# Layer 1 latent keys on token rows: squares, roots and scaling by token, then transposes, with both key slots ahead of the query pairs

## The chip, the cores and the metric

One core of a Trainium2 chip runs the program. The metric is the device time of one execution in microseconds, lower is better. The median of three runs of the kernel before is 1565.3 us (1560.97 to 1568.23).

## What is computed

Two layers of a hybrid backbone over 256 latent and 256 context tokens of 2048 channels. Layer 0 joins windowed attention and a long convolution, layer 1 joins dense grouped attention with multi-head latent attention (MLA). The change is in the keys of MLA, which for latent tokens and context tokens are

```
kv  = (rmsnorm(mkv, ckv_g) @ wukv).reshape(B, L, 8, 128 + 128)   # per head: key part, value part
k_n = rmsnorm(kv[..., :128], mk_g[:128])                          # over the 128 channels of one head, per token
k   = concat([k_n, broadcast(k_r)])                               # k_r: 64 rotated channels, shared by the heads
s   = (q . k) * 192 ** -0.5 ;  o = softmax(s) @ kv[..., 128:]
```

The queries come in the same way from a 512-channel latent, in four pairs of heads, each with a normalised part (qn) and a rotated part (qr). All results are multiplied with a SiLU gate and go through an output projection.

## The kernel before

All tensors are f32. Each product of weights and activations is made of three fp32r products of high and low halves: `split_high` (ScalarE, L979) copies a loaded weight tile `raw` to `wh`, `split_low` (VectorE, L989) makes `wl` as the difference. `raw`, `wh` and `wl` have two buffers each, so tile t+1 is split while tile t is multiplied, and a load (SP queue) starts when the tile two before it is split.

Layer 1 is a hand-written order of `L1_TILES` = 41 slots, one weight tile each. The function `l1_slot(i)` names the fills of a slot; a fill is one accumulation in bank 0 or 1 (`ps[m % 2]`). Every engine walks the slots and does its own part: TensorE the fills, the sums of squares (`sums`), the attention pieces; ScalarE the split of the next tile, the drains of the banks, the roots, exponentials and copies; VectorE the low split, reciprocals, scalings and the softmax. A fill into a bank waits for the drain of the fill two before it (`odd_drained`).

Slots 0 to 18 are the latents, the grouped keys, values and queries and the query latent (cq). From `MLA0` = 19 to slot 30 odd slots hold MLA fills and even slots one gate tile each: slot 19 is kn 0 to 3 and vm 0 to 3 (keys and values of four heads), slots 21 and 23 query pairs 0 and 1, slot 25 the other four heads' keys and values, slots 27 and 29 query pairs 2 and 3. Slots 31 to 40 are gates. `MLA_SLOTS` gives the slot in which each MLA head's attention (units 8 to 15) has its scores; its transposes follow one slot later, its outputs two.

A key fill before (kind kn) has a head's 128 channels on the partitions and 512 tokens on the free axis. So the sum over channels is a product with ones on TensorE. Four heads share one norm: `sums` (L2040) puts the sums of head n on 16 rows of bank 7, one root (L2184) and one reciprocal (L2275, 128x512) serve the four, and `pick` (L2051) is a product that spreads one head's row over all partitions of bank 7, from which `scale_kn` (L2290) scales the key. `PICK_LAG` = 6 sets how many fills later. Bank 7 is shared by the sums, the picks and the swaps of the rotations (`swap`, L2060), so these wait for each other's readers. The latent cq's norm closes at the first fill of slot 19, so its root, its four scalings (L2283) and its splits `cqh` and `cql` (L2243, L2355) fall into that slot.

## Time and profile before

| | |
|---|---|
| median of three runs | 1565.3 us (1560.97 to 1568.23) |
| profiled execution | 1564.63 us, span 1562.8 us |
| TensorE busy | 1482.5 us, 95% |
| VectorE busy | 1025.4 us, 66% |
| ScalarE busy | 575.9 us, 37% |
| mean granted TensorE clock | 0.984 of 2.4 GHz |
| layer 1's slots 19 to 40 | 1235.69 to 1461.35 us of the span |
| output projection of layer 1 | from there to the end |

Times inside the span are counted from its start. TensorE's busy time is modelled at its ends: a matmul's record is longer than the spacing of two, so prices are read from start to start. A whole f32 matmul appears as two records, an fp32r one as one.

### The profile page before, as it was taken

How to read it: one execution, taken by the hardware profiler on the slowest of the kernel's cores; microseconds unless marked ns; L12 is line 12 of the kernel's file. 1: busy time of each engine (PE TensorE's matmuls, PEld its weight loads, DVE VectorE, ACT ScalarE, POOL GpSimd, SP SyncE). 2: the span in 40 equal slices, each digit the busy share in tenths (PEclk: the TensorE clock that was granted, in tenths of full speed). 3: DMA queues.
4: the chain of work that ended last, by engine and by line, in shares of the span. 5: the costliest groups of instructions: out<-in, count | busy, mean ns of one | idle time of the engine just before them, and what ended most of it. 6: DMA issues, size and time to landing. Idle time of an engine off the chain costs nothing.

```text
span 1562.8 us, 19306 instructions
## 1 busy us (share of the span) xinstructions
PE 1482.5 (95%) x7755; PEld 1181.3 (76%) x7755; DVE 1025.4 (66%) x1199; ACT 575.9 (37%) x806; POOL 214.7 (14%) x242
## 2 busy tenths in 40 slices
PE   5978999999999999999998999989999988999998
PEld 1325888888888787788776888877788775788998
DVE  3373898889897876876666545464577465565543
ACT  2543222222222334433234211253367545555332
POOL 1000333322231100000000334430000000000000
PEclk9998999999999999999999999989999999999999
DMA  9996554554654544452548666522232322233563
GB/s 356 380 363 239 205 180 167 166 192 148 216 175 153 200 150 154 135 196 93 193 160 307 211 226 207 190 95 89 101 126 91 101 75 75 74 109 121 193 220 141
DMA packets 72904, 272.29 MB, mean 174 GB/s; under 512 B 11056, under 2 KB 25584, under 8 KB 53104
## 3 DMA queue, kind: packets, MB, share of 16 engines
q1 hardware_dynamic: 52640, 193.45, 35.2%
q0 software_dynamic: 20176, 77.61, 14.3%
q8 instruction: 62, 1.02, 0.3%
q14 instruction: 26, 0.21, 0.0%
HBM read 256.36 MB, written 14.68 MB: 173 GB/s over the span
## 4 chain that ended last, share of the span: by engine, by line
PE 82%; DMA 6%; DVE 4%; ACT 4%; issue 3%; SPq 0%; ACTq 0%; DVEq 0%; POOL 0%
PE banks L1027 20%; PE banks L1028 20%; PE banks L1031 20%; DMA raw<-in_ev_tiles 2%; PE banks L1198 2%; PE banks L1185 2%; PE banks L2110 2%; DMA ada_ring<-in_ada_first 2%; ACT wh L979 1%; DMA spectra<-kstage 1%; PE banks L2040 1%; PE banks L1001 1%; PE banks L538 1%; PE banks L1004 1%; PE banks L1002 1%
## 5 line engine op out<-in xcount | busy, mean ns | idle before, releaser
L1027 PE MATMUL banks<-xh,wh 128*128 128x512 f32 (+1 forms) x1808 | 619.3, 358 | 7.2 <-ACT wh L979 7.2
L1028 PE MATMUL banks<-xl,wh 128*128 128x512 f32 (+1 forms) x1808 | 604.4, 350 | 0.0
L1027 PEld LDWEIGHTS banks<-xh,wh 128*128 128x128 f32 x1808 | 342.8, 190 | 60.7 <-issue 15.9
L1028 PEld LDWEIGHTS banks<-xl,wh 128*128 128x128 f32 x1808 | 343.0, 190 | 46.2 <-issue 3.1
L1031 PE MATMUL banks<-xh,wl 128*128 128x512 f32 (+1 forms) x1808 | 354.9, 349 | 0.0
L989 DVE TENSOR_TENSOR wl<-raw,wh 128x2048 fp32r<-128x2048 f32 (+1 forms) x124 | 281.3, 2269 | 88.1 <-ACT wh L979 88.1
L1031 PEld LDWEIGHTS banks<-xh,wl 128*128 128x128 f32 x1808 | 295.9, 189 | 43.6
L979 ACT ACTIVATE wh<-raw 128x2048 fp32r<-128x2048 f32 (+1 forms) x124 | 235.5, 1900 | 239.5 <-PE banks L1031 169.2
L373 DVE SCALAR_TENSOR_TENSOR ada_acc<-ada_w,cond,ada_acc 128x1024 f32<-128x1024 f32 x120 | 159.3, 1328 | 6.0 <-DMA ada_w<-in_ada_rest 3.9
L396 POOL DMA_DIRECT2D ada_w<-in_ada_rest x128 | 69.0, 539 | 586.8 <-DVE ada_acc L385 390.0
L385 DVE SCALAR_TENSOR_TENSOR ada_acc<-ada_w,cond,ada_acc 128x1024 f32<-128x1024 f32 x90 | 125.3, 1392 | 0.0
L2275 DVE RECIPROCAL rs<-rs 128x256 f32<-128x256 f32 (+1 forms) x27 | 56.9, 2107 | 56.9 <-ACT rs L2184 56.7
L1818 DVE SCALAR_TENSOR_TENSOR hT<-banks,ada,hres 128x256 f32<-128x256 f32 x48 | 21.7, 480 | 103.0 <-PE banks L1031 102.4
L1342 ACT ACTIVATE cx<-banks,cols 128x512 f32<-128x512 f32 x16 | 12.5, 778 | 147.4 <-PE banks L1031 147.4
L1160 POOL TENSOR_TENSOR spec<-spec,prod 128x512 f32<-128x512 f32 x32 | 47.5, 1510 | 55.4 <-DVE prod L1500 55.4
L538 PE MATMUL banks<-ada_ring,condw 128*32 128x512 f32 x256 | 36.0, 645 | 14.0 <-DMA ada_ring<-in_ada_first 9.2
L2309 DVE TENSOR_REDUCE mx<-banks 128x2 f32<-128x1024 f32 x16 | 19.6, 1223 | 32.1 <-PE banks L2090 24.3
L2040 PE MATMUL banks<-sq,core 128*128 128x256 f32 (+1 forms) x74 | 29.3, 478 | 11.7 <-ACT sq L2176 4.7
L1001 PE MATMUL banks<-xh,wh 128*128 128x512 f32 x64 | 27.1, 423 | 14.0 <-DVE wl L989 11.3
L1402 ACT ACTIVATE prob<-banks,nb,qscale 128x512 f32<-128x512 f32 (+1 forms) x32 | 21.2, 667 | 44.4 <-DVE nb L1581 44.4
L2193 ACT ACTIVATE prob<-banks,nb 128x512 f32<-128x512 f32 x32 | 21.7, 684 | 37.1 <-DVE nb L2311 37.1
L1375 ACT ACTIVATE th<-banks 128x512 f32<-128x512 f32 x16 | 9.5, 591 | 66.0 <-PE banks L1031 66.0
(293 smaller groups left out, 1621.9 us busy)
## 6 DMA issues: line engine op xcount, KB each, us to landing
ada_w<-in_ada_rest POOLq DMA_DIRECT2D x128, 512.0 KB, 3.8
raw<-in_ev_tiles SPq DMA_DIRECT2D x52, 1024.0 KB, 6.4
raw<-in_od_tiles SPq DMA_DIRECT2D x34, 1024.0 KB, 4.8
ada_ring<-in_ada_first SPq DMA_DIRECT2D x32, 1024.0 KB, 11.0
raw<-in_out_tiles SPq DMA_DIRECT2D x32, 1024.0 KB, 5.2
hT<-in_hT POOLq DMA_DIRECT2D x4, 1024.0 KB, 11.0
spectra<-kstage POOLq DMA_DIRECT2D x4, 1024.0 KB, 10.5
kf<-spectra SPq DMA_DIRECT2D x8, 512.0 KB, 5.6
```

The lines of the kernel that those rows point to most:

```text
L373: ins = nc.vector.scalar_tensor_tensor(out=acc[:, 0, :], in0=w, scalar=b.cond[:, k, 0:1], in1=acc[:, 0, :], op0=ALU.mult, op1=ALU.add)
L385: ins = nc.vector.scalar_tensor_tensor(out=acc[:, 1, :], in0=w, scalar=b.cond[:, k, 1:2], in1=acc[:, 1, :], op0=ALU.mult, op1=ALU.add)
L396: pool.dma_start(b.ada_w[:, p % 2, :], ada_rest[p // KT, p % KT]).then_inc(s.ada_landed[p % 2], 16)
L538: last = nc.tensor.matmul(ps[7][32 * q:32 * q + 32, :], b.condw[:, 4 * r + q, :], b.ada_ring[p % ADA_RING][:, q // 2, q % 2, :], start=(r ...
L979: nc.scalar.activation(b.wh[:, t % 2, 0:width], b.raw[:, t % 2, 0:width], ACT.Copy).then_inc(s.hi_done, 1)
L989: nc.vector.tensor_tensor(b.wl[:, t % 2, 0:width], b.raw[:, t % 2, 0:width], b.wh[:, t % 2, 0:width].bitcast(F32), ALU.subtract).then_inc( ...
L1027: nc.tensor.matmul(out, wh[:, k, :], b.xh[:, seg, k, :], start=(k == 0), stop=False)
L1028: nc.tensor.matmul(out, wh[:, k, :], b.xl[:, seg, k, :], start=False, stop=False)
L1031: last = nc.tensor.matmul(out, wl[:, k, :], b.xh[:, seg, k, :], start=False, stop=(k == KT - 1))
L1160: nc.gpsimd.tensor_tensor(b.spec[:, j], b.spec[:, j], b.prod[:, j % 2, :].rearrange("p (v c) -> p v c", v=2), ALU.subtract if j % 2 == 0 e ...
L2040: nc.tensor.matmul(ps[7][:, 0:width], lhs.get(kind, b.ones), b.sq1[:, (count_fills(m, NORMED) - 1) % 2, 0:width], start=first, stop=closes ...
L2275: v.reciprocal(b.rs1[:, 0:width], b.rs1[:, 0:width]).then_inc(s.odd_rstd, 1)
```

## The change

- `l1_slot` gives key fills the kind kt: fill kt 4*half + t has the 128 tokens of tile t on the partitions and the channels of four heads side by side on the free axis (tokens as the stationary side, as the value fills have it). The sums (L2040) and picks (L2051) of the keys are gone, and GROUPED has no kn.
- ScalarE copies the bank to `ktok[t]` (which lies in the place of `kn` for heads 4 to 7) and squares it to `sqk`, one buffer. VectorE reduces the squares of each head to one column (`key_squares`, into `kss`). After four tiles ScalarE takes the root of 16 columns (`key_roots`), VectorE the reciprocal, and scales the four tiles by a broadcast of the columns (`scale_keys`).
- TensorE turns the 16 blocks of 128x128 into banks 4 to 7 (`turn_keys`) and ScalarE copies them to `kn` with the gain as scale (`keep_keys`), in the slot after.
- `MLA_AT` sets the order: keys in slots 19 and 21, query pairs in 24, 26, 28 and 30; gates in 20, 22, 23, 25, 27, 29 and from 31. The turns stand at the end of slots 20 and 22. `MLA_SLOTS` goes from (24, 25, 26, 28, 30, 32, 34, 36) to (27, 28, 29, 30, 31, 33, 35, 36).

```diff
     b.cq = put("cq", "U", 20 * K, [P, 4, 256])
+    b.ktok = [b.kn[:, 4 + t, :] for t in range(4)]
+    b.sqk = put("sqk", "U", 62 * K, [P, 512])
+    b.kss = put("kss", "V", 2432, [P, 16])
+    b.krk = put("krk", "V", 2496, [P, 16])
     b.cqh = put("cqh", "U", 24 * K, [P, 4, 256], F32R)
...
 T1 = OUT0 + OUT_TILES
-MLA0 = 19
-NORMED = ("ckv", "kr", "k", "q", "cq", "kn", "qn", "qr")
-PICK_LAG = 6
+MLA_AT = {19: ("k", 0), 21: ("k", 1), 24: ("q", 0), 26: ("q", 1), 28: ("q", 2), 30: ("q", 3)}
+KEY_TURN = {20: 0, 22: 1}
+NORMED = ("ckv", "kr", "k", "q", "cq", "qn", "qr")
 ROTATED = ("kr", "k", "q", "qr")
-GROUPED = {"ckv": 2, "cq": 4, "kn": 4}
+GROUPED = {"ckv": 2, "cq": 4}
 MEAN = {"ckv": 256, "cq": 512, "kr": 64, "qr": 64}
...
         return [("cq", i - 15, 256)]
-    if i < MLA0 + 12 and (i - MLA0) % 2 == 0:
-        half, r = divmod((i - MLA0) // 2, 3)
-        if r == 0:
-            return [("kn", 4 * half + n, T) for n in range(4)] + [("vm", 4 * half + n, T) for n in range(4)]
-        pair = 2 * half + r - 1
-        return [("qn", 2 * pair, 256), ("qn", 2 * pair + 1, 256), ("qr", pair, 256)]
+    if i in MLA_AT:
+        side, n = MLA_AT[i]
+        if side == "k":
+            return [("kt", 4 * n + t, T) for t in range(4)] + [("vm", 4 * n + t, T) for t in range(4)]
+        return [("qn", 2 * n, 256), ("qn", 2 * n + 1, 256), ("qr", n, 256)]
     return [("gate", l1_gate(i), 256)]
...
-    if i >= MLA0 + 12:
-        return i - MLA0 - 6 if i < L1_TILES else None
-    return (i - MLA0) // 2 if i > MLA0 and (i - MLA0) % 2 else None
+    if i < min(MLA_AT) or i in MLA_AT or i >= L1_TILES:
+        return None
+    return i - min(MLA_AT) - sum(at < i for at in MLA_AT)
...
-def group_end(m):
-    return fill_is(m, ("kn",)) and FILLS[m][1] % 4 == 3
 def hurried(m):
...
-MLA_SLOTS = (24, 25, 26, 28, 30, 32, 34, 36)
+MLA_SLOTS = (27, 28, 29, 30, 31, 33, 35, 36)
...
     kind, n, _ = l1_slot(i)[0]
-    if kind == "kn":
+    if kind == "kt":
         return g.od_wukv[0, :, 256 * n:256 * n + 1024].rearrange("(k p) n -> p k n", p=P), (2, 1024)
...
         return b.qo[:, 8 + n, :]
-    return {"ckv": b.ckv, "k": b.kgqa, "v": b.vpre1, "q": b.qo, "cq": b.cq, "kn": b.kn, "qr": b.qr}[kind][:, n, :]
+    return {"ckv": b.ckv, "k": b.kgqa, "v": b.vpre1, "q": b.qo, "cq": b.cq, "qr": b.qr}[kind][:, n, :]
...
                 pe.wait_ge(s.odd_drained, m - 1)
-            if kind in ("kn", "vm", "qn", "qr"):
+            if kind in ("kt", "vm", "qn", "qr"):
                 pe.wait_ge(s.hi_done, t + 1)
                 pe.wait_ge(s.lo_done, t + 1)
-            if kind in ("kn", "vm"):
+            if kind in ("kt", "vm"):
                 pe.wait_ge(s.ckv_high, 2)
...
                     for k in range(2):
-                        if kind == "kn":
-                            lhs, rhs, out = w[wp][:, k, 256 * (n % 4):256 * (n % 4) + P], xp[:, k, :], bank
-                        else:
-                            lhs = xp[:, k, P * (n % 4):P * (n % 4) + P]
-                            rhs = w[wp][:, k, :].rearrange("p (h c) -> p h c", h=4)[:, :, P:2 * P]
-                            out = bank.rearrange("p (h c) -> p h c", h=4)
+                        lhs = xp[:, k, P * (n % 4):P * (n % 4) + P]
+                        side = slice(0, P) if kind == "kt" else slice(P, 2 * P)
+                        rhs = w[wp][:, k, :].rearrange("p (h c) -> p h c", h=4)[:, :, side]
+                        out = bank.rearrange("p (h c) -> p h c", h=4)
                         ins = nc.tensor.matmul(out, lhs, rhs, start=(c == 0 and k == 0), stop=(c == 2 and k == 1))
...
                     pe.wait_ge(s.odd_swap_used, swaps_before(m + 1))
-                if count_fills(m - 1, ("kn",)):
-                    last = max(j for j in range(m) if fill_is(j, ("kn",)))
-                    pe.wait_ge(s.odd_normed, count_fills(last, NORMED))
-            lhs = {"kr": b.blocks64, "qr": b.blocks64, "kn": b.batch[:, 112 - 16 * (n % 4):240 - 16 * (n % 4)]}
+                if kind == "qn":
+                    pe.wait_ge(s.odd_kread, 10)
+            lhs = {"kr": b.blocks64, "qr": b.blocks64}
             nc.tensor.matmul(ps[7][:, 0:width], lhs.get(kind, b.ones),
...
-        def pick(m):
-            n = FILLS[m][1]
-            last = m + 3 - n % 4
-            pe.wait_ge(s.odd_rstd, count_norms(last))
-            if n % 4:
-                pe.wait_ge(s.odd_normed, count_fills(m - 1, NORMED))
-            nc.tensor.matmul(ps[7], b.pick[:, n % 4, :], b.rs1[:], start=True, stop=True).then_inc(s.odd_pick, 1)
+        def turn_keys(half):
+            if half == 0:
+                pe.wait_ge(s.odd_out, 8)
+                pe.wait_ge(s.odd_probT, 8)
+                pe.wait_ge(s.odd_root, count_norms(FIRST_FILL[min(MLA_AT)] - 1))
+                pe.wait_ge(s.odd_swap_used, swaps_before(FIRST_FILL[min(MLA_AT)]))
+            else:
+                pe.wait_ge(s.odd_kread, 6)
+            for t in range(4):
+                pe.wait_ge(s.odd_kmade, 9 * half + 6 + t)
+                for h in range(4):
+                    last = nc.tensor.transpose(ps[4 + t][:, P * h:P * h + P], b.ktok[t][:, P * h:P * h + P], b.ident)
+                last.then_inc(s.odd_kturned, 1)
...
                 pe.wait_ge(s.odd_kr, 1)
+                pe.wait_ge(s.odd_kread, 10)
             if u > 0:
...
                     fill(i, m)
-                if fill_is(m - PICK_LAG, ("kn",)) and not group_end(m - PICK_LAG):
-                    pick(m - PICK_LAG)
                 for r in rotated_at(m):
...
                 scores(l1_unit(i))
-            if group_end(FIRST_FILL[i + 1] - PICK_LAG):
-                pick(FIRST_FILL[i + 1] - PICK_LAG)
+            if i in KEY_TURN:
+                turn_keys(KEY_TURN[i])
             for m in rotated_at(FIRST_FILL[i]):
...
                 return
-            if (kind, n) == ("kn", 0):
+            if (kind, n) == ("kt", 0):
...
                 act.wait_ge(s.odd_scored, 8)
+            if kind == "kt":
+                half, t = divmod(n, 4)
+                if half:
+                    act.wait_ge(s.odd_kturned, t + 1)
+                a.activation(b.ktok[t], bank, ACT.Copy).then_inc(s.odd_kcopied, 1)
+                if n:
+                    act.wait_ge(s.odd_kmade, 9 * half + t if t else 4)
+                a.activation(b.sqk[:], bank, ACT.Square).then_inc(s.odd_drained, 1)
+                return
             if kind not in NORMED:
...
             a.activation(b.sq1[:, q % 2, 0:width], bank, ACT.Square).then_inc(s.odd_drained, 1)
+        def key_roots(half):
+            act.wait_ge(s.odd_kmade, 9 * half + 4)
+            a.activation(b.krk[:], b.kss[:], ACT.Sqrt, scale=1.0 / 128, bias=b.small[:, 0:1]).then_inc(s.odd_kread, 1)
+        def keep_keys(half):
+            for t in range(4):
+                act.wait_ge(s.odd_kturned, 4 * half + (4 if half else t + 1))
+                a.activation(b.kn[:, 4 * half:4 * half + 4, P * t:P * t + P],
+                             ps[4 + t].rearrange("p (h t) -> p h t", h=4), ACT.Copy,
+                             scale=b.cols[:, COL["mk_n"]:COL["mk_n"] + 1]).then_inc(s.odd_kread, 1)
...
                     root(m - 1)
+                if fill_is(m - 2, ("kt",)) and FILLS[m - 2][1] % 4 == 3:
+                    key_roots(FILLS[m - 2][1] // 4)
                 if fill_is(m - 2, ("ckv", "cq")) and closes_norm(m - 2):
...
                 gated_high(l1_gate(i - 1))
+            if i - 1 in KEY_TURN:
+                keep_keys(KEY_TURN[i - 1])
             for m in rotated_at(FIRST_FILL[i - 1]) if i else ():
...
             v.reciprocal(b.rs1[:, 0:width], b.rs1[:, 0:width]).then_inc(s.odd_rstd, 1)
-            if kind == "kn":
-                return
             dve.wait_ge(s.odd_rstd, count_norms(m))
...
-        def scale_kn(m):
-            n = FILLS[m][1]
-            dve.wait_ge(s.odd_pick, n + 1)
-            dve.wait_ge(s.odd_kept, count_fills(m, NORMED))
-            v.scalar_tensor_tensor(out=b.kn[:, n, :], in0=b.kn[:, n, :], scalar=b.cols[:, COL["mk_n"]:COL["mk_n"] + 1],
-                                   in1=ps[7], op0=ALU.mult, op1=ALU.mult).then_inc(s.odd_normed, 1)
+        def key_squares(m):
+            half, t = divmod(FILLS[m][1], 4)
+            dve.wait_ge(s.odd_drained, m + 1)
+            if half and t == 0:
+                dve.wait_ge(s.odd_kread, 1)
+            v.tensor_reduce(b.kss[:, 4 * t:4 * t + 4], b.sqk[:].rearrange("p (h c) -> p h c", h=4), AX.X,
+                            ALU.add).then_inc(s.odd_kmade, 1)
+        def scale_keys(half):
+            dve.wait_ge(s.odd_kread, (1, 2)[half])
+            v.reciprocal(b.krk[:], b.krk[:]).then_inc(s.odd_kmade, 1)
+            dve.wait_ge(s.odd_kmade, 9 * half + 5)
+            dve.wait_ge(s.odd_kcopied, 4 * half + 4)
+            for t in range(4):
+                x = b.ktok[t].rearrange("p (h c) -> p h c", h=4)
+                v.tensor_tensor(x, x, b.krk[:, 4 * t:4 * t + 4].unsqueeze(2).to_broadcast([P, 4, P]),
+                                ALU.mult).then_inc(s.odd_kmade, 1)
...
             for m in range(FIRST_FILL[i], FIRST_FILL[i + 1]):
-                if fill_is(m - PICK_LAG, ("kn",)) and not group_end(m - PICK_LAG):
-                    scale_kn(m - PICK_LAG)
+                if fill_is(m - 1, ("kt",)):
+                    key_squares(m - 1)
+                if fill_is(m - 3, ("kt",)) and FILLS[m - 3][1] % 4 == 3:
+                    scale_keys(FILLS[m - 3][1] // 4)
                 for r in rotated_at(m):
...
                 gated_low(l1_gate(i - 1))
-            if group_end(FIRST_FILL[i + 1] - PICK_LAG):
-                scale_kn(FIRST_FILL[i + 1] - PICK_LAG)
             for m in rotated_at(FIRST_FILL[i]):
```

Three places show how instructions stand. TensorE, the start of slot 19, before (`wh`, `wl`: weight halves, `ckvh`, `ckvl`: latent halves, `sq` with `core`: a sum of squares):

```order
L2007 MATMUL banks<-ckvl,wh 128x512 x2
L2007 MATMUL banks<-ckvh,wl 128x512 x2
L2040 MATMUL banks<-sq_158,core 128x256
L2007 MATMUL banks<-ckvh,wh 128x512 x2
L2007 MATMUL banks<-ckvl,wh 128x512 x2
L2007 MATMUL banks<-ckvh,wl 128x512 x2
L2040 MATMUL banks<-sq_158,core 128x512
L2007 MATMUL banks<-ckvh,wh 128x512 x2
L2007 MATMUL banks<-ckvl,wh 128x512 x2
```


and with the change:

```order
L2003 MATMUL banks<-wh,ckvl 128x512 x2
L2003 MATMUL banks<-wl,ckvh 128x512 x2
L2035 MATMUL banks<-sq_158,core 128x256
L2003 MATMUL banks<-wh,ckvh 128x512 x2
L2003 MATMUL banks<-wh,ckvl 128x512 x2
L2003 MATMUL banks<-wl,ckvh 128x512 x2
L2003 MATMUL banks<-wh,ckvh 128x512 x2
L2003 MATMUL banks<-wh,ckvl 128x512 x2
L2003 MATMUL banks<-wl,ckvh 128x512 x2
```


The sum of cq's squares stays behind the first fill; the sums of 512 columns between the key fills are gone, and fill follows fill.

ScalarE, slot 19, before (`kn`: the copy of a key fill, `sq`: its square, `rs`: the root of cq's norm, `cqh`: high halves of cq):

```order
L2172 ACTIVATE kn<-banks 128x512
L2176 ACTIVATE sq_158<-banks 128x512
L2184 ACT_TABLE_LOAD
L2184 ACTIVATE rs_151<-banks,small 128x256
L2172 ACTIVATE kn<-banks 128x512
L2176 ACTIVATE sq_158<-banks 128x512
L2243 ACTIVATE cqh<-cq 128x256 x4
L2172 ACTIVATE kn<-banks 128x512
L2176 ACTIVATE sq_158<-banks 128x512
L2172 ACTIVATE kn<-banks 128x512
L2176 ACTIVATE sq_158<-banks 128x512
```


and with the change, where each square but the first waits for `key_squares` on VectorE:

```order
L2173 ACTIVATE kn<-banks 128x512
L2176 ACTIVATE sqk<-banks 128x512
L2204 ACT_TABLE_LOAD
L2204 ACTIVATE rs_151<-banks,small 128x256
L2173 ACTIVATE kn<-banks 128x512
L2176 ACTIVATE sqk<-banks 128x512
L2265 ACTIVATE cqh<-cq 128x256 x4
L2173 ACTIVATE kn<-banks 128x512
L2176 ACTIVATE sqk<-banks 128x512
L2173 ACTIVATE kn<-banks 128x512
L2176 ACTIVATE sqk<-banks 128x512
```


The order is the same, the square's buffer is now `sqk`, and the waits differ.

ScalarE, from the gate of slot 20 to the first query pair in slot 21, before:

```order
L2160 ACT_TABLE_LOAD
L2160 ACTIVATE silu_153<-banks 128x256
L2161 ACTIVATE silu_153<-banks 128x256
L979 ACTIVATE wh<-raw 128x2048
L2172 ACTIVATE qo<-banks 128x256
L2176 ACTIVATE sq_158<-banks 128x256
L2172 ACTIVATE qo<-banks 128x256
```


and with the change from the gate of slot 23 to the first query pair in slot 24:

```order
L983 ACTIVATE wh<-raw 128x1536
L2160 ACTIVATE silu_153<-banks 128x256
L2161 ACTIVATE silu_153<-banks 128x256
L2238 ACTIVATE xh<-qo 128x256
L2194 ACTIVATE kn<-banks,cols 128x4x128 x4
L983 ACTIVATE wh<-raw 128x2048
L2181 ACTIVATE qo<-banks 128x256
L2185 ACTIVATE sq_158<-banks 128x256
L2181 ACTIVATE qo<-banks 128x256
L2185 ACTIVATE sq_158<-banks 128x256
```


The copies of the second half's keys (L2194) stand between the gate's drain and the split of the next tile (L983), behind which the first query fill is drained.

## Rows read from the trace of the kernel before

**Rows 1.** The page, part 1: busy time, share of the span, instructions of each engine.

```profile
PE 1482.5 (95%) x7755; PEld 1181.3 (76%) x7755; DVE 1025.4 (66%) x1199; ACT 575.9 (37%) x806; POOL 214.7 (14%) x242
```

**Rows 2.** Windows: length, PE, PEld, DVE, ACT, POOL busy (instructions), PEclk, DMA, GB/s.

```profile
1235.69:1260.02 24.33, 20.39 (x73) 13.98 (x71) 11.99 (x13) 13.00 (x21) 0.00 (x0) 0.93 0.24 74
...
1303.55:1328.84 25.29, 20.66 (x78) 13.00 (x77) 10.85 (x14) 13.93 (x21) 0.00 (x0) 1.00 0.18 62
1328.84:1384.17 55.33, 51.62 (x318) 42.67 (x317) 35.95 (x45) 32.52 (x59) 0.00 (x0) 0.97 0.27 91
1384.17:1461.35 77.18, 77.18 (x570) 70.12 (x568) 44.34 (x62) 38.87 (x63) 0.00 (x0) 1.00 0.36 125
```

**Rows 3.** Timeline of TensorE, slot 19: start, us, operation, count, [idle before <-releaser].

```profile
1234.89 1.04 PE L2100 MATMUL banks<-core,prob 128*128 128x128 f32 x8
1235.69 0.71 PE L2007 MATMUL banks<-ckvh,wh 128*128 128x512 f32 x2
...
1250.08 1.02 PE L2040 MATMUL banks<-sq,core 128*128 128x512 f32 x2
...
1251.41 0.62 PE L2007 MATMUL banks<-wh,ckvl 128*128 128x512 f32 x2
1251.87 0.62 PE L2007 MATMUL banks<-wl,ckvh 128*128 128x512 f32 x2
```

**Rows 4.** Timeline of TensorE, slots 19 to 27: the waits, and two pairs in between.

```profile
1241.65 1.45 PE L2040 MATMUL banks<-sq,core 128*128 128x512 f32 x2 [2.51 <-issue]
...
1243.75 1.06 PE L2007 MATMUL banks<-ckvl,wh 128*128 128x512 f32 x2
1244.60 1.06 PE L2007 MATMUL banks<-ckvh,wl 128*128 128x512 f32 x2
...
1255.27 1.13 PE L2051 MATMUL banks<-rs,core 128*128 128x512 f32 x2 [1.43 <-DVE rs L2275]
...
1267.91 1.10 PE L2051 MATMUL banks<-rs,core 128*128 128x512 f32 x2 [0.93 <-DVE kn L2290]
...
1308.79 1.12 PE L2040 MATMUL banks<-sq,core 128*128 128x512 f32 x2 [2.15 <-ACT sq L2176]
...
1321.88 1.12 PE L2051 MATMUL banks<-rs,core 128*128 128x512 f32 x2 [2.48 <-DVE rs L2275]
...
1346.76 0.67 PE L2040 MATMUL banks<-sq,core 128*128 128x256 f32 x2 [1.75 <-DVE kn L2290]
```

**Rows 5.** Timeline of VectorE, slot 19: the scaling of cq.

```profile
1243.38 1.67 DVE L2283 SCALAR_TENSOR_TENSOR cq<-cq,cols,rs 128x256 f32<-128x256 f32 x4
```

**Rows 6.** Groups by line and shape, VectorE and ScalarE, whole span: busy, mean ns, idle before.

```profile
L1573 DVE TENSOR_REDUCE mx<-banks 128x2 f32<-128x512 f32 x8 | 5.5, 684 | 1.9 <-PE banks L1254 1.9
...
L821 DVE TENSOR_TENSOR xl<-nu,xh 128x512 fp32r<-128x512 f32 x16 | 11.1, 692 | 0.5
...
L979 ACT ACTIVATE wh<-raw 128x2048 fp32r<-128x2048 f32 x120 | 229.6, 1913 | 239.5 <-PE banks L1031 169.2 <-DMA raw<-in_ev_tiles 50.4 <-DMA spectra<-kstage 12.2
```

**Rows 7.** Timeline of ScalarE, slot 19.

```profile
1239.79 1.28 ACT L2184 ACT_TABLE_LOAD   x1
...
1241.45 0.59 ACT L2172 ACTIVATE kn<-banks 128x512 f32<-128x512 f32 x1
...
1245.08 1.33 ACT L2243 ACTIVATE cqh<-cq 128x256 fp32r<-128x256 f32 x4 [2.55 <-DVE cq L2283]
```

**Rows 8.** Timeline of TensorE: the swap behind slot 22, and slot 29's first sum to last.

```profile
1284.17 1.22 PE L2060 MATMUL banks<-qr,core 128*128 128x256 f32 x2 [2.87 <-DVE qr L2283]
...
1368.25 0.89 PE L2040 MATMUL banks<-sq,core 128*128 128x256 f32 x2 [1.96 <-ACT sq L2176]
...
1371.51 0.83 PE L2040 MATMUL banks<-sq,core 128*128 128x256 f32 x2
```

**Rows 9.** Timeline of VectorE, unit 10 in slot 28: the maximum and the scaled probabilities.

```profile
1362.84 1.22 DVE L2309 TENSOR_REDUCE mx<-banks 128x2 f32<-128x1024 f32 x1 [1.73 <-PE banks L2090]
...
1365.99 0.88 DVE L2316 TENSOR_SCALAR prob<-prob,rden 128x512 f32<-128x512 f32 x2
```

More of the change, by code:

```diff
@@ L2452, in semaphores @@
     s.odd_out = sem("odd_out")
-    s.odd_pick = sem("odd_pick")
+    s.odd_kcopied = sem("odd_kcopied")
+    s.odd_kmade = sem("odd_kmade")
+    s.odd_kread = sem("odd_kread")
+    s.odd_kturned = sem("odd_kturned")
     s.odd_prob = sem("odd_prob")
```

## The prediction

> **What bounds the kernel now.** I read the page first: TensorE is busy for 1482.5 us, 95% of the span, VectorE for 66% and ScalarE for 37% [rows 1]. So only work taken off TensorE, or TensorE's own waits, can move the time. Next the windows, cut at the edges of layer 1's slots: idle is length less PE busy [rows 2]. Slot 19 (keys and values of heads 0 to 3) takes 24.33 us with 3.9 idle, slot 25 with slot 26's attention pieces (heads 4 to 7) 25.29 with 4.6 idle, slots 27 to 30 lose 3.7 of 55.33. From slot 31 on nothing is idle in 77.18 us. The change touches the two latent key slots and the order of the slots up to 30; behind them TensorE is the bound and passes on whatever was won.
>
> **What goes from TensorE.** The eight L2040 sums of 512 columns and the eight L2051 picks. At full clock L2040 starts at 1250.08 and the pair behind the next one at 1251.41: 1.33 us for it and one L2007 pair, and a pair alone takes 0.46 (1251.41 to 1251.87). So an f32 matmul of 512 columns costs 0.87 us [rows 3]; the picks have the same shape. 16 x 0.87 = 13.9 us.
>
> **What comes to TensorE.** 32 transposes of 128x128. Eight of the kernel's L2100 transposes take 0.80 us from start to the next operation's start (1234.89 to 1235.69) [rows 3], 0.10 each: 3.2 us. Net work: 13.9 - 3.2 = **-10.7 us**. The kt fills are the same six matmuls of 512 columns as the kn fills, with the operands' sides exchanged as the vm fills have them; L2007 has the same spacing in both forms, so they cost nothing.
> The Trainium skill (TensorE: Matmul & The Clock Gate, "Part 4: PE-mode transpose") gives about 275 ns for one transpose in a kernel. By that the 32 would cost 8.8 us and the net would be -5.1; the row's 0.10 us decides, and the rule is rival 3.
>
> **Waits that go.** (a) Slot 19: the sum of kn 0 stood behind the root of the last cq on bank 7 (2.51 us idle before 1241.65), and the clock was then at 1.2 GHz: a pair took 0.85 (1243.75 to 1244.60) instead of 0.46, some 1.5 us over the three fills' pairs that ran slow [rows 4, 3]. The first pick waited 1.43 for the reciprocal. (b) Slot 20: 0.93 before the fourth pick. (c) Slot 25: 2.15 before a sum and 2.48 before a pick. (d) Slot 27: 1.75 before qn's sum, which waited for the last key scaling [rows 4]. Together **-12.8 us**.
>
> **Waits that come.** (e) *Slot 19.* sqk is one buffer, so ScalarE's square of kt 1 waits until VectorE has reduced the square of kt 0, and that reduce is queued behind the cq normalise, whose four scalings end at 1243.38 + 1.67 = 1245.05 [rows 5]. A reduce of 128x512 to four columns: the nearest row is 0.68 [rows 6]. ScalarE copies the second key tile at 1241.45 as before, stands to about 1245.75 for the square, is done at 1246.3, and makes the four cqh (1.33 us) [rows 7]. TensorE meanwhile: kt 2 needs kt 0's drain, whose square is over when the table load behind it starts at 1239.79 [rows 7], and ends at 1241.2 (three pairs of 0.46); kt 3 needs kt 1's drain. So TensorE idles about 0.8 and then **5.1 us**, and restarts at 1246.4 at the slow clock (the 2.51 us gap here was enough for that). kt 3 slow takes 2.7, to 1249.1; kt 2's square, behind the cqh and a reduce, lets vm 0 go at 1249.5 and costs 0.5, and vm 0 half slow 0.6. Then vm 1, 2, 3 at 1.4 each and the outputs of unit 7 with 1.7 (four f32 matmuls of 256 columns, half of 0.87 each) put gate 0 at 1257.5, where it stood at 1260.02 [rows 2]. Stalls here: 7.0 us.
> (f) *Slot 21.* ScalarE and VectorE alternate: square 0.5, reduce 0.65, two handovers of 0.1, against 1.37 of TensorE a fill. About 0.4 at kt 7's bank, another 0.4 behind: 0.8 us. The DVE reciprocal of 16 columns replaces one of 512 (3.35) and the scalings of four tiles (nearest row 0.69 each [rows 6]) end before turn_keys: slot 20's and slot 22's gates (48 matmuls of 256 columns at 0.12, half of 0.23, 5.8 us each) cover root, reciprocal and scalings, about 3.5 us. turn_keys(1) also needs keep_keys(0), 4 x 0.5 on ScalarE at the head of slot 22: ready some 2.5 us early. If that cover went, it would cost 1 to 3.
> (g) *Slot 24*, the first query pair. ScalarE leaves gate 2 at 1290.6 by my walk and then makes xh (0.3, a quarter of the four cqh), the four keep_keys (2.0, near four of the 0.59 copies of rows 7, which overlap a little as the cqh do) and the split of the next tile (1.9 [rows 6]) before it drains qn 0 with 0.55, at 1295.4. TensorE, with gate 2 ended at 1290.0, has filled qn 0 and qn 1 (24 matmuls at 0.12) by 1292.9: 2.5 us idle, then slow. The price of a slow stretch after such a gap is in slot 29: 1368.25 to 1371.51 at the slow clock, 3.26 us, of which I count 1.3 as lost [rows 8]. 2.5 + 1.3 = 3.8.
> (h) *Slot 28*, the third pair, now follows a slot with exponentials (unit 8), as slot 29 did before (1.96 idle, then slow [rows 8]): 3.2 us. Slot 30 does the same as slot 29 before: no change. The swap behind the first pair, with no attention to cover it, still waits 2.87 [rows 8]: moved to slot 25, no change.
> Together e to h: 7.0 + 0.8 + 3.8 + 3.2 = **+14.8 us**.
>
> **The other moves.** Units 8 to 15 go to slots 27 to 36, later and denser. No SP transfer is added; tiles load in the new order, each when the split two tiles earlier is done, and slots 22 and 23 as gates give them time. POOL has no part in it. ScalarE gains four table loads net (1.28 us each [rows 7], 5.1 in all); they lie in slots 26 to 31. There ScalarE has, by my count, about 18 us of work in each 22 us of TensorE: I cost them at nothing, unless that cover is gone (rival 2).
>
> **Sum.** -10.7 - 12.8 + 14.8 = **-8.7 us**; the small waits inside the first pair that (g) swallows make it **-9**. The profiled execution took 1564.6 (span 1562.8 and 1.8 around it), 0.7 under the median of 1565.3. 1564.6 - 9 = 1555.6; against the median 1556.3. I say **1556**. About 0.5% (7.8 us) is what a measurement of this kernel can tell from no change; the bound for faster is 1557.5.
> Bounds. Low: if (e) idles only the 2.5 us it had before and (h) does not come, -15. High: if (e), (g) and (h) each last 2 us more, -3.
>
> **The rivals.**
> *1. The stalls take the gain back.* The wait (e) grows since the clock stays low over the value fills too, and (g) and (h) are each a full slow stretch as behind the swap at 1284.17. For it: three new waits, each on ScalarE. Against: TensorE loses 13.9 us of work for certain. -3, so 1562.
> *2. Slower: dense units.* Slots 27 to 31 carry a unit each. If the chain from the maximum to the scaled probabilities (1362.84 to 1365.99 + 0.88, 4.0 us [rows 9]), now with table loads between, is not covered, TensorE waits for it at the transposes: five slots x 4.0 = 20, so -9 + 20 = +11, 1576. It decides when less than 4.0 us of TensorE work, plus 1.3 for a load, stands between scores and transposes. Against: a gate gives 5.8, a pair 5.2 (36 matmuls at 0.12 and two sums at 0.43), and three units in a row in slots 24 to 26 had no such wait.
> *3. Dear transposes.* If a key transpose takes 0.28 us and not 0.10, 32 of them give back 5.6: 1561. The transposed operand is the moving one in both, so I hold it unlikely.
> *4. Cheap waits.* The clock does not fall and (e) is short: 1550.
> That the change would not do what it says is no case: the order shows the sums and picks gone.
>
> **Chances.** Forecast (1553 to 1560) 0.60, rival 1 0.22, rival 2 0.06, rival 3 0.05, rival 4 0.07. Faster by over 0.5%: three quarters of the forecast's case and rival 4, 0.52. Slower: rival 2 and a little, 0.07. Same: 0.41. The range 1550 to 1563 leaves out rival 2 and some of the ends.
>
> **What would show it.** In the new profile: no f32 matmul of 512 columns in the key slots beside the fills; two groups of 16 transposes of 0.1 us; gate 0's product at about 1257.5; a gap near 5 us in slot 19 before the fourth key fill, released by the square; a gap near 2.5 us in slot 24; slot 21 at about 11.5 us where slot 25 had some 21.6 without attention. I am wrong if slot 19 ends later than 1260, if slot 21 has gaps over 2 us, or if the slots from 32 on show idle.

## The result and the profile after

The changed kernel takes **1552.77 us** (median of six runs, 1550.41 to 1556.17), the kernel before, run beside it, 1564.97: a ratio of 0.9926 with a 95% interval of 0.9906 to 0.9945. The forecast was 1556 (1550 to 1563). The profiled executions took 1564.63 and 1556.17.

The page's first line, which answers to [rows 1]:

```profile
PE 1473.7 (95%) x7755; PEld 1177.9 (76%) x7755; DVE 1024.1 (66%) x1207; ACT 585.2 (38%) x818; POOL 217.0 (14%) x242
```

TensorE has 8.8 us less of busy time and the same share. The two profiled executions differ by less than the medians, since the profiled execution of the change came 2.9 us later to slot 19 (1238.63, before 1235.69), before any changed instruction; in the profiles below this point lies between 1233.95 and 1238.17. So I compare the stretch from the first key fill of slot 19 to the first matmul of the output projection. Windows of that stretch, before and after (columns as in [rows 2]):

```profile
1235.69:1462.10 226.41, 207.51 (x1277) 172.83 (x1275) 131.86 (x161) 123.87 (x206) 0.00 (x0) 0.97 0.30 99
```

```profile
1238.63:1453.53 214.90, 197.65 (x1277) 169.85 (x1274) 130.43 (x169) 132.93 (x218) 0.00 (x0) 0.97 0.31 104
1238.63:1260.84 22.21, 16.60 (x62) 12.44 (x59) 12.46 (x19) 12.73 (x21) 0.00 (x0) 0.85 0.25 93
1268.45:1280.32 11.87, 11.65 (x52) 8.64 (x50) 5.59 (x8) 8.82 (x15) 0.00 (x0) 1.00 0.37 115
```

It went from 226.41 to **214.90 us, 11.5 less**, which is nearly the difference of the medians (12.2). Slot 19 took 22.21 where it took 24.33 [rows 2], the second key slot 11.87 alone where it took 25.29 with 3.7 us of attention in it. TensorE waits in slot 19 in fewer places, but longer. Its timeline there:

```profile
1242.76 0.73 PE L2003 MATMUL banks<-wh,ckvh 128*128 128x512 f32 x2 [0.68 <-ACT sqk L2176]
...
1243.79 0.62 PE L2003 MATMUL banks<-wl,ckvh 128*128 128x512 f32 x2
1249.27 1.22 PE L2003 MATMUL banks<-wh,ckvh 128*128 128x512 f32 x2 [4.86 <-ACT sqk L2176]
1250.28 1.06 PE L2003 MATMUL banks<-wh,ckvl 128*128 128x512 f32 x2
1251.14 1.06 PE L2003 MATMUL banks<-wl,ckvh 128*128 128x512 f32 x2
...
1266.78 1.91 PE L2051 MATMUL banks<-core,kn 128*128 128x128 f32 x16
1268.45 0.70 PE L2003 MATMUL banks<-wh,ckvh 128*128 128x512 f32 x2
```

The wait of 4.86 us stands before the fourth key fill, and the clock is at its lower level behind it: a pair takes 0.86 us (1250.28 to 1251.14), where it took 0.46 at 2.4 GHz [rows 3], and the mean granted clock of the slot is 0.85, where it was 0.93 [rows 2]. The 16 turns take 1.67 us, 0.104 each. The waits of the query pairs in slots 24, 28 and 30, and of the swap in slot 25:

```profile
1299.53 1.01 PE L2035 MATMUL banks<-sq,core 128*128 128x256 f32 x2 [2.84 <-ACT sq L2185]
...
1312.70 0.70 PE L2061 MATMUL banks<-qr,core 128*128 128x256 f32 x2 [2.87 <-DVE qr L2305]
...
1335.45 0.67 PE L2035 MATMUL banks<-sq,core 128*128 128x256 f32 x2 [1.84 <-ACT sq L2185]
...
1359.25 0.67 PE L2035 MATMUL banks<-sq,core 128*128 128x256 f32 x2 [1.97 <-ACT sq L2185]
```

And what ScalarE and VectorE do during the long wait:

```profile
1244.39 0.59 ACT L2173 ACTIVATE kn<-banks 128x512 f32<-128x512 f32 x1
1248.62 0.60 ACT L2176 ACTIVATE sqk<-banks 128x512 f32<-128x512 f32 x1 [3.64 <-DVE kss L2313]
1249.11 1.32 ACT L2265 ACTIVATE cqh<-cq 128x256 fp32r<-128x256 f32 x4
```

```profile
1244.53 1.75 DVE L2299 RECIPROCAL rs<-rs 128x256 f32<-128x256 f32 x1 [0.47 <-ACT rs L2204]
1246.31 1.67 DVE L2305 SCALAR_TENSOR_TENSOR cq<-cq,cols,rs 128x256 f32<-128x256 f32 x4
1247.90 0.68 DVE L2313 TENSOR_REDUCE kss<-sqk 128x4 f32<-128x512 f32 x1
```

ScalarE has copied the second token tile at 1244.39 and stands until 1248.62, since the reduce of the first square (`kss`, at 1247.90, 0.68 us) is behind the reciprocal and the scalings of cq in VectorE's queue.

### The profile page after: what moved, and what is told of

The parts are those of the page before. It is cut to its first block, busy times and chain, and to the rows that moved or that the text cites. A ratio compares the mean times of both kernels' runs of the same rounds, so it can differ in the third digit from the quotient of the medians.

```text
span 1554.3 us, 19313 instructions
## 1 busy us (share of the span) xinstructions
PE 1473.7 (95%) x7755; PEld 1177.9 (76%) x7755; DVE 1024.1 (66%) x1207; ACT 585.2 (38%) x818; POOL 217.0 (14%) x242
## 4 chain that ended last, share of the span: by engine, by line
PE 82%; DMA 6%; ACT 4%; DVE 4%; issue 3%; SPq 1%; DVEq 0%; ACTq 0%; POOL 0%
PE banks L1031 20%; PE banks L1032 20%; PE banks L1035 20%; DMA raw<-in_ev_tiles 2%; PE banks L1202 2%; PE banks L1189 2%; DMA ada_ring<-in_ada_first 2%; PE banks L2112 2%; ACT wh L983 1%; DMA spectra<-kstage 1%; PE banks L1005 1%; PE banks L2035 1%; PE banks L542 1%; PE banks L1008 1%; PE banks L1006 1%
## 5 line engine op out<-in xcount | busy, mean ns | idle before, releaser
L993 DVE TENSOR_TENSOR wl<-raw,wh 128x2048 fp32r<-128x2048 f32 x124 | 281.3, 2269 | 92.0 <-ACT wh L983 92.0
L983 ACT ACTIVATE wh<-raw 128x2048 fp32r<-128x2048 f32 x124 | 235.7, 1901 | 237.1 <-PE banks L1035 170.4
L1822 DVE SCALAR_TENSOR_TENSOR hT<-banks,ada,hres 128x256 f32<-128x256 f32 x48 | 21.8, 481 | 104.0 <-PE banks L1035 103.5
L2299 DVE RECIPROCAL rs<-rs 128x256 f32<-128x256 f32 (+1 forms) x25 | 50.2, 2008 | 41.5 <-ACT rs L2204 41.3
L1005 PE MATMUL banks<-xh,wh 128*128 128x512 f32 x64 | 27.1, 424 | 13.9 <-DVE wl L993 11.2
L1157 POOL TENSOR_TENSOR fold<-cz 128x512 f32<-128x512 f32 x16 | 28.4, 1794 | 34.8 <-DVE cz L1529 25.9
```

The costliest lines, as they stand in the source:

```text
L983: nc.scalar.activation(b.wh[:, t % 2, 0:width], b.raw[:, t % 2, 0:width], ACT.Copy).then_inc(s.hi_done, 1)
L993: nc.vector.tensor_tensor(b.wl[:, t % 2, 0:width], b.raw[:, t % 2, 0:width], b.wh[:, t % 2, 0:width].bitcast(F32), ALU.subtract).then_inc( ...
L1005: nc.tensor.matmul(out, wh[:, k, :], b.xh[:, :, k, :], start=(k == 0), stop=False)
L2299: v.reciprocal(b.rs1[:, 0:width], b.rs1[:, 0:width]).then_inc(s.odd_rstd, 1)
```

## The experiments

Medians of four to ten runs (the change: six); the stretch is that from slot 19's first key fill to the output projection's first matmul, in one profile of each kernel. Two kernels whose intervals overlap are not told apart by their medians. The kernel before, in the runs beside them, had 1564.64 us (the first four), 1565.18 (the next three) and 1566.38 (the last four).

| kernel | us | ratio to before, 95% | stretch us |
|---|---|---|---|
| before | 1564.97 | | 226.41 |
| the change | 1552.77 | 0.9926 (0.9906 to 0.9945) | 214.90 |
| order alone | 1562.38 | 0.9986 (0.9975 to 0.9998) | 224.24 |
| four buffers of squares | 1552.69 | 0.9919 (0.9896 to 0.9942) | 212.76 |
| cq's norm later | 1546.20 | 0.9876 (0.9854 to 0.9899) | 208.64 |
| no norm of the keys | 1544.74 | 0.9877 (0.9854 to 0.9901) | 207.46 |
| key copies earlier | 1549.50 | 0.9903 (0.989 to 0.9917) | 208.61 |
| splits later | 1552.42 | 0.992 (0.9907 to 0.9934) | 214.19 |
| these four together | 1546.23 | 0.9888 (0.987 to 0.9906) | 207.57 |
| rotation earlier | 1554.35 | 0.9931 (0.9916 to 0.9947) | 215.04 |
| rotation earlier, two splits later | 1546.58 | 0.9877 (0.9857 to 0.9897) | 210.86 |
| all mended | 1541.24 | 0.9847 (0.983 to 0.9865) | 202.09 |
| the removed work put back | 1566.99 | 1.0005 (0.9991 to 1.002) | 228.46 |

**The order alone.** The kernel before, keys as they were, with the change's tables:

```diff
-MLA0 = 19
+MLA_AT = {19: ("k", 0), 21: ("k", 1), 24: ("q", 0), 26: ("q", 1), 28: ("q", 2), 30: ("q", 3)}
...
-MLA_SLOTS = (24, 25, 26, 28, 30, 32, 34, 36)
+MLA_SLOTS = (27, 28, 29, 30, 31, 33, 35, 36)
```

> The kernel before with the new order of slots and attention units alone; keys as before (sums, picks, one root of four heads). Theory (the gain is the 10.7 us of TensorE work that went, and the waits only changed places): the key slots keep their waits on bank 7, so about the time before, 1562 to 1568. Rival (the order makes the gain, since both key slots come before the query pairs): 1556 or less.

It took 1562.38. Its stretch:

```profile
1235.13:1459.37 224.24, 206.83 (x1277) 171.48 (x1275) 132.08 (x161) 128.78 (x210) 0.00 (x0) 0.98 0.30 100
```

224.24 us: by the stretch the order gives 2.2 of the 11.5 us, the token keys 9.3. The order's part was not in the sum; it is small, and 1.1 of the 2.2 is a slow stretch of the clock behind the first swap that was shorter in this profile (see "The key copies earlier").

**No norm of the keys.** The same kernel with the order, and the latent keys' norm left out altogether:

```diff
-NORMED = ("ckv", "kr", "k", "q", "cq", "kn", "qn", "qr")
+NORMED = ("ckv", "kr", "k", "q", "cq", "qn", "qr")
-PICK_LAG = 6
+PICK_LAG = 6000
```

> Leaves the norm of the latent keys out in the kernel with the new order: no squares, sums, roots, picks, scalings or transposes of keys. What it is faster than e1 is the price of the old norm, what it is faster than the change is the price of the new one. Theory: old norm 13.9 us of TensorE work and some 5 of waits, 18 to 20 us over e4; new norm 3.3 us of transposes, 2.4 of key copies before the query pair and 2 of waits, 7 to 8 us over e4, so e4 at 1545. Rival (the token norm is nearly free and the order pays): e4 within 4 us of the change.

1544.74 us, and the stretch is 207.46:

```profile
1233.95:1441.41 207.46, 193.76 (x1246) 166.63 (x1244) 119.82 (x151) 120.55 (x198) 0.00 (x0) 0.97 0.32 108
```

The old norm costs 224.24 - 207.46 = 16.8 us, the new one 214.90 - 207.46 = 7.4. By the medians they are 17.6 and 8.0. The new one is as expected (7 to 8), the old one a little under 18 to 20. In this profile the stretch behind the first swap was 1.2 us longer than in the two it is compared with, so both prices are rather too small than too large. Even here slot 19 keeps a wait of 3.20 us before the first value fill: the drain of the third key fill is behind the four `cqh`, and these are behind cq's scalings. That part of slot 19's wait belongs to cq, not to the keys:

```profile
1244.73 1.22 PE L2006 MATMUL banks<-wh,ckvh 128*128 128x512 f32 x2 [3.20 <-ACT kn L2169]
```

**The removed work, put back.** 16 f32 matmuls of 512 columns in front of the turns:

```diff
                 pe.wait_ge(s.odd_kmade, 9 * half + 6 + t)
+                for _ in range(2):
+                    nc.tensor.matmul(ps[4 + t], b.ones, b.ktok[t], start=True, stop=True)
```

> The changed kernel with 16 more f32 matmuls of 512 columns, two ahead of each token tile's turn in slots 20 and 22 (their results are overwritten by the turns). It is the work of the eight sums and eight picks that the change took away, at a place without waits. Theory: 16 x 0.87 us, 13.9 us slower than the change, 1566 to 1567. Rival (such work hides behind other engines there): under 7 us.

1566.99 us. That is 14.2 over the change, and the stretch grows by 13.6. Read in place, slot 20's eight and its turns take 8.54 us (1262.16 to 1270.70) where the turns alone took 1.67, so 0.86 for each. The stretch:

```profile
1234.92:1463.38 228.46, 211.55 (x1309) 175.94 (x1307) 130.50 (x169) 132.94 (x218) 0.00 (x0) 0.96 0.30 98
```

So the work of the sums and picks, 0.85 us a matmul here, is on the path in full, and with it the change gains nothing.

**Four buffers for the squares.** `sqk` becomes a list of four, and the square's wait for the reduce falls away in slot 19 (the cut shows the buffers alone).

```diff
-    b.sqk = put("sqk", "U", 62 * K, [P, 512])
+    b.sqk = [put(f"sqk{j}", "U", k * K, [P, 512]) for j, k in enumerate((62, 58, 56, 54))]
```

> The changed kernel with four buffers for the squares, so that ScalarE's square no longer waits for VectorE's reduce. Theory (the 4.86 us wait before the fourth key fill is the queue on VectorE and ScalarE behind the norm of cq): the wait before the fourth fill goes, but the next fill waits for the drain of the third, which is behind the four cqh; 1 to 2 us faster than the change, 1551. Rival (the single buffer is the cause of the wait): 5 us or more, 1548.

1552.69 us, the change's time; the expected gain of 1 to 2 us is not shown. Its stretch is 2.1 us shorter, but only 0.55 of that are waits of slot 19, and slot 19 as a whole differs by up to 1.5 us between profiles of kernels with the same code there (see below). The timeline of TensorE shows the wait cut in two, not gone:

```profile
1245.06 0.73 PE L2003 MATMUL banks<-wh,ckvh 128*128 128x512 f32 x2 [1.11 <-ACT sqk L2176]
...
1249.92 1.22 PE L2003 MATMUL banks<-wh,ckvh 128*128 128x512 f32 x2 [3.20 <-ACT sqk L2176]
```

1.11 before the fourth key fill and 3.20 before the first value fill, the same 3.20 as without any norm. Together they are 4.31 against 4.86: the single buffer held the fourth fill longer, but most of what it held back would have waited here.

**The norm of cq later.** The steps of cq's root, scalings and splits become functions of the fill:

```diff
+def root_step(m):
+    return m + (7 if FILLS[m][0] == "cq" else 1)
+def norm_step(m):
+    return FIRST_FILL[22] if FILLS[m][0] == "cq" else m + 1
```

> The changed kernel with the root of cq's norm put behind the key roots in slot 19, its reciprocal and scalings in slot 22 and its two splits in slot 23; one buffer of squares as in the change. Theory: slot 19 shrinks from 22.2 us to about 16, the 4.86 us wait and the slow clock behind it go; 5 to 7 us faster than the change, 1546. Rival (ScalarE's split and drains bound the slot, and the time comes back later): within 2 us of the change, with the waits in slots 20 to 24.

1546.20 us, 6.6 faster than the change. What is left in slot 19 and what came in slot 24:

```profile
1242.29 0.73 PE L2018 MATMUL banks<-wh,ckvh 128*128 128x512 f32 x2 [0.93 <-ACT sqk L2191]
...
1286.49 0.71 PE L2029 MATMUL banks<-cqh,wh 128*128 128x256 f32 x4 [2.61 <-DVE cql L2407]
```

The 4.86 us are 0.93. cq's low half now lands late for the first query pair and holds it for 2.61, since in slot 23 I had put its splits behind gate 2's drain. That costs almost nothing new: it stands in the place of the change's 2.84 us before the same pair's sum, where no wait is left. TensorE waits a little earlier, and ScalarE works off its key copies and its split meanwhile.

**The key copies earlier.** `keep_keys(1)` goes from the end of slot 23 to behind that slot's split, where ScalarE was idle:

```diff
+            if KEY_TURN.get(i - 1) == 1:
+                keep_keys(1)
...
-            if i - 1 in KEY_TURN:
-                keep_keys(KEY_TURN[i - 1])
+            if KEY_TURN.get(i - 1) == 0:
+                keep_keys(0)
```

> The changed kernel with the second half's four key copies (keep_keys) moved from behind gate 2's drain in slot 23 to ahead of it, where ScalarE stood idle for 5.2 us. Theory: the 2.84 us wait in slot 24 falls to about 0.5, and the slow clock behind it may go: 2.3 to 3.6 us faster than the change, 1549 to 1550.5. Rival (the split of the next tile alone holds the drain): the wait stays over 2 us, no difference.

1549.50 us; the stretch is 6.3 less than the change's, the median 3.3, as expected (2.3 to 3.6), though the two intervals of the table overlap a little. The wait fell as expected, by 2.32:

```profile
1294.79 0.70 PE L2035 MATMUL banks<-sq,core 128*128 128x256 f32 x2 [0.52 <-ACT sq L2185]
...
1306.89 0.70 PE L2061 MATMUL banks<-qr,core 128*128 128x256 f32 x2 [2.87 <-DVE qr L2307]
...
1313.05 0.67 PE L2035 MATMUL banks<-sq,core 128*128 128x256 f32 x2 [0.73 <-issue]
```

The rest is clock. The pair behind the shorter wait runs 1.1 us faster (first sum to swap, 12.10 against 13.17). That belongs to the wait: the three kernels with 0.52 or 0.53 us of it have 12.1 there, the five with 2.83 or 2.84 have 12.9 to 14.4. From the swap to the sum at 1313.05 are 6.16 us; in the change, from the swap at 1312.70 to the sum at 1320.34, 7.64. The wait of 2.87 before the swap is the same in both, and only in the change is there a stretch at 1.2 GHz behind it. The windows, the change's first:

```profile
1312.70:1320.34 7.64, 6.92 (x41) 6.64 (x41) 4.15 (x7) 4.58 (x8) 0.00 (x0) 0.78 0.45 140
```

```profile
1306.89:1313.05 6.16, 5.43 (x41) 5.15 (x41) 4.16 (x7) 4.59 (x8) 0.00 (x0) 1.00 0.47 117
```

These 1.5 us can't be put down to the edit. The order alone and the kernel without a key norm have the short wait in slot 24 too, and take 7.67 and 8.88 us behind the swap. And the kernel with the early rotation (below) keeps the wait of 2.83 and takes 6.16:

```profile
1311.96 0.70 PE L2061 MATMUL banks<-qr,core 128*128 128x256 f32 x2 [2.87 <-DVE qr L2305]
...
1318.12 0.67 PE L2035 MATMUL banks<-sq,core 128*128 128x256 f32 x2 [0.73 <-issue]
```

All thirteen profiles have this swap with its 2.87 us of waiting and the same TensorE work behind it, and from it to the next pair's second sum are 6.16 us in four of them, 7.64 to 7.68 in six and 8.78 to 8.88 in three. The last 1.4 us lie in slot 19, ahead of the edit: with the same code and the same waits it took 22.21 in the change and 20.76 here (20.8 to 22.2 in the six profiles that have this code). So about 3.4 of the 6.3 us are the edit's, which is what the medians show.

**The splits later.** In the pair slots, the split of the next tile goes behind the first two drains and the first root:

```diff
+            pair_slot = FILLS[FIRST_FILL[i]][0] == "qn"
-            if i > 1:
+            if i > 1 and not pair_slot:
                 split_high(nc, act, b, s, t0 + i + 1, width(i + 1))
...
+                if pair_slot and m == FIRST_FILL[i] + 1:
+                    split_high(nc, act, b, s, t0 + i + 1, width(i + 1))
```

> The changed kernel where, in the four query pair slots, the split of the next weight tile stands behind the drains of the first two fills and the first root (ScalarE) or its reciprocal (VectorE). Theory: the waits of 1.84 and 1.97 us in slots 28 and 30 go, and the one in slot 24 falls from 2.84 to about 1: 4 to 7 us faster than the change, 1547. Rival (the split is then late for the next gate, or the roots wait instead): under 2 us, with a new wait at the gate's first product.

1552.42 us, no gain: this expectation was wrong in slots 28 and 30. Slot 24's wait did fall, from 2.84 to 1.03. TensorE's timeline:

```profile
1297.00 0.36 PE L1031 MATMUL banks<-xh,wh 128*128 128x256 f32 x1 [1.17 <-ACT wh L983]
...
1315.82 0.36 PE L1031 MATMUL banks<-xh,wh 128*128 128x256 f32 x1 [1.17 <-ACT wh L983]
...
1332.01 0.67 PE L2035 MATMUL banks<-sq,core 128*128 128x256 f32 x2 [1.82 <-DVE rope L2337]
...
1355.40 0.67 PE L2035 MATMUL banks<-sq,core 128*128 128x256 f32 x2 [1.97 <-DVE rope L2337]
```

The waits of slots 28 and 30 stand at 1.82 and 1.97 as before, but now it is the rotation on VectorE that ends them (L2337): bank 7 still holds the swap of the pair before. Two waits ended nearly together, and the profile had named the later one. In slots 25 and 27 the split is now late for the gate (1.17 each).

**Four together**: the edits above for cq's norm, the four buffers, the key copies and the splits in one kernel.

> The late cq norm, four buffers of squares, early key copies and late splits together. Theory (the waits are separate places on TensorE's path, so they add): 6.5 + 2 for the third pair and fourth pair each + 2.8 in slot 24, 12 to 14 us faster than the change, 1540. Rival (one wait takes the place of another): 8 us or less, 1545.

1546.23 us, 6.5 under the change and no better than the late cq norm alone (1546.20): the rival's case. Two of its waits:

```profile
1285.11 0.71 PE L2029 MATMUL banks<-cqh,wh 128*128 128x256 f32 x4 [2.61 <-DVE cql L2415]
...
1292.65 0.36 PE L1031 MATMUL banks<-xh,wh 128*128 128x256 f32 x1 [1.17 <-ACT wh L983]
```

Against the late cq norm alone the 0.93 in slot 19 is gone, but the late splits bring 1.17 in slot 25 and again in slot 27, and the 2.61 in slot 24, the 1.82 in slot 28 and the 1.97 in slot 30 stand. The early key copies had nothing left to win, since with the late norm no wait stands before that pair's first sum.

**The rotation earlier**: inside the softmax, while ScalarE makes the exponentials.

```diff
+            for r in turned:
+                rotate(r)
             dve.wait_ge(s.odd_exped, 2 * (u + 1))
             v.reciprocal(b.rden[:], b.rowsum[:]).then_inc(s.odd_rden, 1)
```

> The changed kernel where VectorE rotates the query pair while ScalarE makes the exponentials (behind the maximum and its scale) instead of behind the whole softmax and gate. Theory (in slots 28 and 30 the first sum waits for two things that end together: the square, late behind the split, and bank 7, late behind the rotation): alone it gives nothing in slots 28 and 30, both waits stay at 1.8 to 2.0 with the square as releaser; within 1 us of the change. Rival (the rotation was the only wait): 3 to 4 us faster.

1554.35 us, the change within its spread; the stretch is 215.04. **With the late split in slots 28 and 30 alone** (the edit as against the late split above):

```diff
-            pair_slot = FILLS[FIRST_FILL[i]][0] == "qn"
+            pair_slot = FILLS[FIRST_FILL[i]][0] == "qn" and l1_unit(i) is not None
```

> The early rotation and, in slots 28 and 30 alone, the late split. Theory (both waits must go at once): the two waits of 1.8 and 2.0 fall to under 0.5 each; 3 to 4 us faster than the change. Rival (a third wait stands behind them, the maximum or the exponentials): under 1.5 us.

1546.58 us, 6.2 under the change (four runs from 1544.47 to 1551.72, so the 6.2 is loose), and 4.0 in the stretch. TensorE in slots 28 and 30, first with the rotation alone, then with both (there the first and the second sum of each pair):

```profile
1333.10 0.70 PE L2035 MATMUL banks<-sq,core 128*128 128x256 f32 x2 [1.70 <-ACT sq L2185]
...
1356.92 0.70 PE L2035 MATMUL banks<-sq,core 128*128 128x256 f32 x2 [1.86 <-ACT sq L2185]
```

```profile
1332.00 0.70 PE L2035 MATMUL banks<-sq,core 128*128 128x256 f32 x2
...
1334.69 0.67 PE L2035 MATMUL banks<-sq,core 128*128 128x256 f32 x2 [0.57 <-issue]
...
1354.34 0.70 PE L2035 MATMUL banks<-sq,core 128*128 128x256 f32 x2
...
1356.88 0.67 PE L2035 MATMUL banks<-sq,core 128*128 128x256 f32 x2 [0.42 <-issue]
```

Neither mend alone moves the waits of the first sums by more than 0.2; with both they are gone, and 0.57 and 0.42 stand before the second sums. From the swap ahead of each pair to the next attention piece behind it are 6.7 us where the change took 8.2 and 8.3, so 3.2 us together, within the 3 to 4 expected. The rest of the 4.0 lies ahead of slot 28, where the code is the change's.

**The version with all of it**: late cq norm with its splits ahead of gate 2's drain, ring, early key copies, early rotation, late splits in slots 28 and 30. New beside the edits above is one, in ScalarE's fills (`highs` makes `cqh`):

```diff
+                if gate_slot:
+                    highs(m)
                 drain(m)
```

> Late cq norm with its splits ahead of gate 2's drain in slot 23, four buffers of squares, early key copies, early rotation, and late splits in slots 28 and 30 alone. Theory: over the late cq norm alone (1546.2) it wins the 2.6 us wait for cql in slot 24 and the 3.7 of slots 28 and 30: 1539 to 1541, and in its profile no wait over 1 us is left between slot 19 and the end but the 2.87 of the swap in slot 25. Rival (slow clock stretches or new waits give it back): 1544 or more.

**1541.24 us** (1539.48 to 1542.90): 25 us under the kernel before and 11.5 under the change, the fastest version here. Its stretch and its two longest waits:

```profile
1238.15:1440.24 202.09, 194.04 (x1277) 167.72 (x1275) 130.03 (x169) 132.69 (x218) 0.00 (x0) 0.98 0.33 111
```

```profile
1285.94 0.71 PE L2029 MATMUL banks<-cqh,wh 128*128 128x256 f32 x4 [1.12 <-DVE cql L2423]
...
1301.35 1.22 PE L2076 MATMUL banks<-qr,core 128*128 128x256 f32 x2 [2.87 <-DVE qr L2333]
```

202.09 us. Left is the swap's 2.87, and 1.12 for cq's low half, which the expectation had at under 1.

## Why the prediction was right, and where it was off

The direction, the mechanism and the range held. The sizes of the clock's part did not, and that they moved within the range is in part luck. Step by step, each against the stretch from slot 19 on:

- *Work removed*, 13.9 us forecast: put back, it costs 13.6 in the stretch. Right.
- *Transposes*, 3.2 forecast: two groups of 16 at 1.67, 3.3. Rival 3 is out: the 32 turns' records are 273 ns in the mean, as the row below shows, but they overlap, and what TensorE pays is the 0.104 from start to start. The Trainium skill (TensorE: Matmul & The Clock Gate, Part 4: PE-mode transpose) gives about 275 ns for a transpose in a kernel. The trace agrees with that as the length of one record and not as the price.

```profile
L2051 PE MATMUL banks<-core,kn 128*128 128x128 f32 x32 | 3.8, 273 | 0.0
```

- *(e) slot 19*: waits of 0.8 and 5.1 forecast, 0.68 and 4.86 measured; the slot 21.8 forecast, 22.21 measured. My reading of what stood behind cq's norm is what the late cq norm confirmed. But I called it the price of the single buffer; most of it (3.20, which the kernel without a key norm has too) is the queue behind `cqh`, which the new keys only inherit.
- *(f) slot 21*: 0.8 over its fills forecast, 11.87 - 8 x 1.37 = 0.9 measured.
- *(g) slot 24*: 2.5 forecast, 2.84 measured, with the slow clock behind it as forecast. The four copies take 2.3 us, not 2.0.
- *(h) slots 28 and 30*: waits of 1.84 and 1.97, as forecast. **Here the sizes were off.** I charged a slow stretch of 1.3 us in slot 28 and kept the one that slot 29 had before; in the change no slow clock followed either wait. By my prices that is 2.6 us of gain not forecast. For slot 28 this is firm: of the eight kernels in which the square ends this wait (1.70 to 1.84; the change is one), none is slow behind it. For slot 30 it is in part luck: three of these eight (the order alone, the early rotation, the removed work put back) take 1.2 to 1.3 us more from that wait to the next swap. The slow stretch behind the first swap was 1.1 shorter (swap to the second sum of the next pair: 7.64, before 8.78, from 1284.17 to 1292.95, the row below), and that is luck too: it is the stretch with three lengths above. With the 0.4 and 0.3 that e and g took more, -8.7 becomes about -11.7, against 11.5 measured; single profiles are not exact enough to make more of this agreement.

```profile
1292.95 0.67 PE L2040 MATMUL banks<-sq,core 128*128 128x256 f32 x2 [0.72 <-issue]
```

- *Rival 1* (the waits give it back) is out, and *rival 2* (dense units) too: no transposes waited for a softmax in slots 27 to 31. ScalarE gained three table loads (26 against 23 over the roots, the exponentials and the gates), not four. But the density does cost: the exponentials of units 8 and 10, with the split behind them, and the rotation behind the softmax are what the two pairs in slots 28 and 30 wait for.

What stays open is when the clock falls behind a wait. Waits of 1.84 and 1.97 in the change were followed by full speed, 1.96 before by a slow stretch [rows 8]; the 2.87 before the swap was followed by none in four profiles and by one of 1.5 or 2.7 us of loss in nine. So single profiles differ by 1 to 3 us on this alone, and a gain of that size has to be read from medians.

## What to carry to other kernels

Work taken off the engine that bounds was worth its start-to-start spacing in full here; waits on other engines mostly moved, and each new place has to be walked through the queues of all engines. Before a wait is mended, ask what else would end within a microsecond of its releaser: here the split and the rotation each hid the other, and only both mends together paid. And before a gain in one profile is put down to an edit, look for the same stretch in the kernels that don't have the edit. And a step whose consumer has moved to a later slot (cq's norm) should move with it: that was worth 6.3 us of the stretch, two thirds of the 9.3 of the key rewrite.

## What the runs showed of the hardware

- A sum over a whole tile on TensorE in f32 costs 0.87 us for 512 columns [rows 3], a turn of 128x128 0.104 from start to start: 16 turns (1.67 us in slot 20) are as dear as two such sums.
- A table load on ScalarE took 1.28 us and the root behind it started at once (1242.72 and 1244.02 in the change):

```profile
1242.72 1.28 ACT L2204 ACT_TABLE_LOAD   x1
1244.02 0.47 ACT L2204 ACTIVATE rs<-banks,small 128x256 f32<-128x256 f32 x1
```

- The same wait of 2.87 us before the same swap, with the same TensorE work behind it, was followed by 6.16, 7.64 to 7.68 or 8.78 to 8.88 us, with a mean granted clock of 1.00, 0.78 and 0.66 in the early key copies, the change and the kernel before. What decides between them no run here shows.
